# A chunked recurrent mixer regrouped on one Trainium2 core: one chunk and both head parities per group, level products on 64x64 quarters

## The chip, the cores and the metric

The kernel runs on one core of one Trainium2 chip. The metric is the device time of one execution in microseconds (us). Three executions of the kernel before took 1795.15, 1797.66 and 1800.07 us; the median is 1797.66.

## The reference

Four mixing layers of width 2048 run over 256 positions, all in float32. The first layer is the one that the change touches. It projects the input (`hn @ w_in`), computes a sparse attention for 8 heads on one part of the columns, and on another part a recurrence over time for 16 heads of width 64 with a state of 64 by 64 per head:

```python
def step(state, inp):
    r_t, w_t, k_t, v_t, a_t, b_t = inp
    sa = jnp.einsum('bhij,bhj->bhi', state, a_t)
    state = (state * w_t[:, :, None, :] + sa[..., None] * b_t[:, :, None, :]
             + v_t[..., None] * k_t[:, :, None, :])
    return state, jnp.einsum('bhij,bhj->bhi', state, r_t)
...
mix = jnp.concatenate([o_a * jax.nn.silu(z_a), o_b * jax.nn.silu(z_b)], axis=-1)
y = mix @ w_out[l]
```

The later layers (a differential attention and a gated linear attention, with their projections) are the same in both kernels.

## The kernel before

Six weight products (an input and an output projection for three layers) make up most of the work. `Gemm` cuts each into chunks of 256 columns and each chunk into four pieces of 512 KB. SyncE loads a piece, ScalarE rounds it (`hi`, L208), VectorE makes the remainder (`lo`, L213), and TensorE runs three matmuls for each *slot*: one 128-row slice of the contraction and one 128-wide tile of the output (L241 to L243, or L250 to L252). A piece of 256 columns has 8 slots. The input projection of the first layer has 992 slots.

Everything else is cut into *stages* that are woven into these slots. Each engine runs a generator that yields at each stage (`pe_stages`, `act_stages`, `dve_stages`), and a table `at` that `stage_slots` fills (L753) gives the slot before which stage n is issued, the same for all three engines. So a table of slots, and no scheduler, sets the order on every engine's queue; semaphores do the rest. Stages whose slot number lies past the last slot are issued after the projection, one after the other (`drained`). The sparse attention has its own table, `nsa_slots` (L351), which starts from the end of the recurrent stages (`at[-5]`): its first stage lies 16 slots behind it, and its last 229 slots behind it. In the kernel before the recurrent stages end at slot 834, so the attention's table runs from 850 to 1063; 17 of its stages lie past slot 992.

The recurrent mixer works in chunks of 128 positions (two chunks, `ch` 0 and 1) and on 8 heads at a time (`hh` 0 and 1). Four tiles `u` of 128 channels hold two heads each: the head of parity 0 on partitions 0 to 63, that of parity 1 on 64 to 127. For each `hh` there is a preparation (16 stages), then two groups of 36 stages, then 4 closing stages. A group takes one parity and *both* chunks; its stages alternate between chunk 0 and chunk 1, and lie 3 slots apart. In a group, for each of the 4 heads of that parity:

- `products` (L1003) makes five 128x128 matrices from 64-row operands: two whose masked parts NL and MU, MT start an inversion, and AK, RB, RK.
- The inversion of a 128x128 triangular matrix goes in `LV` = 6 levels. Each level doubles the size of the diagonal blocks that are inverted (b = 2, 4, ... 64) by two products. The first is NL times the odd block columns of MU (L1042), masked into QQ by VectorE (L1357). The second is MT, the transpose of MU, times QQ (L1052), which VectorE adds to MU (L1367). From level 1 on, TensorE also transposes MU (L1035) and ScalarE copies the result into MT (L1205). At levels 0 to 4 all products use the whole array: weights of 128x128, and 128 (levels 0 and 1) or 64 moving columns. Level 5 joins the two 64x64 halves and uses one 64x64 part (L1030, L1039, L1052).
- The output stages: AK times the values (L1064), MU times that (L1070), the state after chunk 0 (L1078, L1079, L1373 on VectorE), and the result (L1082, L1086, L1088). Chunk 1 also multiplies with the state (L1061, L1082).

Each float32 matmul of these is two instructions in the profile (a weight load and a matmul twice), called *runs* below. The stages that belong together are a *half-stage* of one chunk each:

```python
for lv in range(LV):
    for c in range(2):
        pe.wait_ge(dv_[c], d0[c] + 8 + 2 * lv)
        ...
        yield
    for c in range(2):
        pe.wait_ge(dv_[c], d0[c] + 9 + 2 * lv)
        ...
        yield
```

After the last group, `k.half_done` reaches 2 and SyncE may load the attention's weights and bias tables over the mixer's room. The gate values of the attention half (`za`) go through Silu on ScalarE before its heads start (L569 to L578); those of the recurrent half (`z2`, L1130) follow their projection chunks, and GpSimd multiplies them in (L1480). The block of the first layer ends with a barrier of all engines; then the next layer starts with a rounding of its operand (L1565, L1569) and its first pieces.

## Time and profile before

| what | value |
|---|---|
| median of 3 executions | 1797.66 us |
| the profiled execution: span from first to last instruction | 1793.7 us |
| TensorE busy (matmul) | 1719.0 us, 96% |
| VectorE / ScalarE busy | 1002.4 / 788.1 us |
| mean granted clock of TensorE | 0.981 |
| matmul instructions | 13621 |

The profiled execution's own time is given by its span alone; the median of the executions is 3.96 us longer than that span. The page gives busy time by engine, the granted TensorE clock in slices, DMA queues, the chain that ended last, and the costliest groups of instructions. Since matmuls are pipelined, one that is listed with 1.05 us can be followed by the next after 0.81 us; what a piece of work costs TensorE is read from start to start in the timeline.

### The profile page before, as it was taken

What the parts mean: (1) busy time and instruction counts of PE and PEld (TensorE: products, weight loads), DVE (VectorE), ACT (ScalarE), POOL (GpSimd) and SP (SyncE); (2) the same over time, 40 slices, a digit from 0 to 9 for tenths busy, and PEclk for the clock granted to TensorE, in tenths of its full rate; (3) what the DMA queues carried; (4) which work ended last, traced back from release to release, by engine and by line L of the source; (5) the groups of instructions that cost most, each with busy time, mean ns of one, the idle gap of its engine ahead of it and who ended that gap; (6) DMA issues with size and microseconds to landing.
All of it is one profiled execution on the core that took longest, in us unless ns stands there. A gap on an engine that the chain in (4) does not pass through costs nothing. (4 is left out here: it accounts for less than half of the span.)

```text
span 1793.7 us, 31345 instructions
## 1 busy us (share of the span) xinstructions
PE 1719.0 (96%) x13621; PEld 1639.8 (91%) x13621; DVE 1002.4 (56%) x1273; ACT 788.1 (44%) x1123; POOL 97.4 (5%) x88
## 2 busy tenths in 40 slices
PE   8999999899999898979999999999899999999899
PEld 7989998799998798978999989999898999999899
DVE  5665443664545265466454468887545854455443
ACT  6542223522222355444343348876436434444432
POOL 2210000300000000031000000000011000000000
PEclk9999999899999999989999999999999999999999
DMA  9643232433234915536666534444554655556363
GB/s 283 188 127 94 72 95 60 126 98 92 74 95 120 201 48 172 176 105 174 182 178 168 155 118 139 144 142 153 160 165 135 186 163 146 154 161 181 129 202 104
DMA packets 253584, 254.00 MB, mean 142 GB/s; under 512 B 9153, under 2 KB 249826, under 8 KB 253064
## 3 DMA queue, kind: packets, MB, share of 16 engines
q1 hardware_dynamic: 252792, 251.80, 47.9%
q8 instruction: 107, 1.75, 0.4%
q0 software_dynamic: 656, 0.21, 0.1%
q14 instruction: 29, 0.24, 0.0%
HBM read 249.29 MB, written 2.69 MB: 140 GB/s over the span
## 5 line engine op out<-in xcount | busy, mean ns | idle before, releaser
L213 DVE TENSOR_TENSOR w_lo<-w_raw,w_hi 128x1024 fp32r<-128x1024 f32 (+1 forms) x452 | 550.2, 1220 | 534.1 <-ACT w_hi L208 533.5
L241 PE MATMUL ps<-xt,w_hi 128*128 128x256 f32 x2736 | 805.8, 295 | 24.4 <-DVE w_lo L213 20.5
L242 PE MATMUL ps<-xt,w_hi 128*128 128x256 f32 x2736 | 779.7, 285 | 0.0
L243 PE MATMUL ps<-xt,w_lo 128*128 128x256 f32 x2736 | 779.2, 285 | 0.0
L208 ACT ACTIVATE w_hi<-w_raw 128x1024 fp32r<-128x1024 f32 (+1 forms) x452 | 470.2, 1045 | 667.1 <-PE ps L243 514.9
L241 PEld LDWEIGHTS ps<-xt,w_hi 128*128 128x128 f32 x2736 | 530.0, 194 | 49.5 <-issue 34.8
L242 PEld LDWEIGHTS ps<-xt,w_hi 128*128 128x128 f32 x2736 | 530.6, 194 | 1.2 <-issue 0.7
L243 PEld LDWEIGHTS ps<-xt,w_lo 128*128 128x128 f32 x2736 | 529.9, 194 | 0.0
L250 PE MATMUL ps<-w_hi,xt 128*128 128x256 f32 x832 | 244.0, 293 | 0.0
L251 PE MATMUL ps<-w_lo,xt 128*128 128x256 f32 x832 | 236.8, 285 | 0.0
L252 PE MATMUL ps<-w_hi,xt 128*128 128x256 f32 x832 | 236.6, 284 | 0.0
L250 PEld LDWEIGHTS ps<-w_hi,xt 128*128 128x128 f32 x832 | 161.2, 194 | 8.9 <-issue 7.8
L251 PEld LDWEIGHTS ps<-w_lo,xt 128*128 128x128 f32 x832 | 161.3, 194 | 0.5 <-issue 0.2
L252 PEld LDWEIGHTS ps<-w_hi,xt 128*128 128x128 f32 x832 | 160.9, 193 | 0.0
L319 DVE TENSOR_TENSOR proj<-ps,rs_bc 128x512 f32<-128x512 f32 (+1 forms) x71 | 48.0, 676 | 54.0 <-PE ps L243 53.8
L1052 PE MATMUL ps<-arena 128*128 128x64 f32 (+2 forms) x384 | 46.4, 263 | 0.0
L1052 PEld LDWEIGHTS ps<-arena 128*128 128x128 f32 (+1 forms) x384 | 43.6, 182 | 1.1
L1357 DVE TENSOR_TENSOR arena<-ps,con 128x256 f32<-128x256 f32 (+1 forms) x40 | 21.2, 530 | 38.6 <-PE ps L1042 38.4
L1205 ACT ACTIVATE arena<-ps 128x512 f32<-128x512 f32 x32 | 19.0, 595 | 53.5 <-PE ps L1035 53.3
L1765 ACT ACTIVATE df_sc<-df_sc,df_st 128x128 f32<-128x128 f32 x64 | 28.4, 445 | 7.7 <-DVE df_st L1841 7.6
L1866 DVE RECIPROCAL t_sq<-t_sq 128x256 f32<-128x256 f32 x16 | 27.9, 1746 | 1.0 <-ACT t_sq L1779 1.0
L1472 POOL COPY arena<-con 8x512 f32<-8x512 f32 x2 | 1.3, 667 | 389.7 <-PE ps L1097 389.7
(395 smaller groups left out, 1531.4 us busy)
## 6 DMA issues: line engine op xcount, KB each, us to landing
w_raw<-in_a_w_in SPq DMA_DIRECT2D x128, 512.0 KB, 3.7
w_raw<-in_w_in SPq DMA_DIRECT2D x120, 512.0 KB, 3.6
w_raw<-in_b_w_in SPq DMA_DIRECT2D x96, 512.0 KB, 3.7
w_raw<-in_w_out SPq DMA_DIRECT2D x32, 512.0 KB, 4.2
w_raw<-in_a_w_out SPq DMA_DIRECT2D x32, 512.0 KB, 4.5
w_raw<-in_b_w_out SPq DMA_DIRECT2D x32, 512.0 KB, 3.5
arena<-in_x SPq DMA_DIRECT2D x4, 512.0 KB, 7.1
w_raw<-in_w_in SPq DMA_DIRECT2D x8, 256.0 KB, 3.8
```

Source lines behind the costliest of these rows:

```text
L208: k.nc.scalar.activation(k.wh[:, p % RING, :, 0:w], k.raw[:, p % RAW, :, 0:w], ACT.Copy).then_inc(k.hi_made, 1)
L213: k.nc.vector.tensor_tensor(k.wl[:, p % RING, :, 0:w], k.raw[:, p % RAW, :, 0:w], k.wh[:, p % RING, :, 0:w].bitcast(F32), ALU.subtract).th ...
L241: pe.matmul(os, h[:, cs], xt[:, kt, 0:S], start=st and ct == 0, stop=False, skip_group_check=True)
L242: pe.matmul(os, h[:, cs], xt[:, kt, S:2 * S], start=False, stop=False, skip_group_check=True)
L243: last = pe.matmul(os, l[:, cs], xt[:, kt, 0:S], start=False, stop=sp, skip_group_check=True)
L250: pe.matmul(os, xh, h[:, 0:w], start=st and tt == 0, stop=False, skip_group_check=True)
L251: pe.matmul(os, xh, l[:, 0:w], start=False, stop=False, skip_group_check=True)
L252: last = pe.matmul(os, xl, h[:, 0:w], start=False, stop=sp, skip_group_check=True)
L319: k.nc.vector.tensor_tensor(spec["dst"], g.bank(c)[:, 0:nt * S].rearrange("p (j t) -> p j t", j=nt), view(k.rsb[:, 0:1], [[0, nt], [1, S]] ...
L1052: m = pe.matmul(share(bank(c, 0), u, lv)[half, :], unit(buf[c][MT], u)[half, half], share(buf[c][QQ], u, lv)[half, :], start=True, stop=True)
L1765: nc.scalar.activation(sc[:, i % 2, t, rows[tt]], sc[:, i % 2, t, rows[tt]], ACT.Exp, bias=st[:, i % 2, 0, t, tt:tt + 1], accum_out=st[:, ...
L1866: nc.vector.reciprocal(rh, rh).then_inc(l4, 1)
```

## The change

- **Groups.** A group now takes one chunk and both parities: chunk 0 first, then chunk 1. It has 18 stages instead of 36, and each stage does for parity 0 and 1 what two stages did for chunk 0 and 1. The gaps between stages come from `GROUP_GAPS` (3, 2, 3, 9, then fourteen of 5): 87 slots for a group instead of 108. The recurrent stages end at slot 750 instead of 834, and the attention's table runs from 766 to 979.
- **Products.** The products from 64-row operands take parity 0 and 1 in turn, into two PSUM banks. RK, AK and RB are made in two further banks (4 and 5) by `side_products`: RK before the levels, AK behind the second half of level 1, RB behind the second half of level 3.
- **Levels 0 to 4** work on the two diagonal 64x64 quarters `q` of each matrix: two matmuls with 64 rows and 64 weight columns instead of one with 128 and 128. The quarter q = 0 uses rows 0 to 63 and writes partitions 0 to 63, q = 1 uses and writes 64 to 127, in the same PSUM bank. The moving columns are 64 at levels 0 and 1 and 32 at levels 2 to 4. On VectorE the masked copy into QQ covers 256 or 128 columns, and the addition into MU becomes two operations of 64 partitions for each parity.
- **Level 5 and the output stages** keep their products; matmuls of the two parities that write 64 partitions each now alternate.
- **The gates** `za` of the attention go through Silu later: the first four heads' before the first head, the other four within the stages of head 2.
- The constants array loses 575 columns, most of them masks (`K_END`).

```diff
-LV, ODD = 6, 2
 R_LORA, R_RVK, R_ZB = 0, 1, 28
-N_PE = tuple(5 + 3 * LV - 1 + 4 - c for c in range(2))
-N_DVE = tuple(8 + 2 * LV + 1 - c for c in range(2))
+LV = 6
+G_PE = tuple(2 + 3 * LV - 1 + 4 - ch for ch in range(2))
+G_DVE = tuple(5 + 3 * LV - 1 + 1 - ch for ch in range(2))
 N_ACT = LV - 1 + 3
+GROUP_GAPS = (3, 2, 3, 9) + (5,) * (2 * LV - 1) + (5, 5, 5)
...
-        for _ in range(2 * (12 + 4 * LV)):
-            now += 3
+        for gap in GROUP_GAPS + GROUP_GAPS:
+            now += gap
...
+        def gated(f):
+            za = k.proj[:, T_ZA + 4 * f:T_ZA + 4 * f + 4, :]
+            act.wait_ge(k.evac_d, self.za_done[f])
+            nc.scalar.activation(za, za, ACT.Silu).then_inc(self.zs, 1)
...
+            def products(banks, lhs, rhs, done):
                 for u in range(4):
-                    m = pe.matmul(bank(c, y)[:, u * P:(u + 1) * P], lhs[ps_, u, cs], rhs[ps_, u, cs],
-                                  start=True, stop=True)
-                m.then_inc(mm_[c], 1)
-
-            for c in range(2):
-                if par == 0:
-                    pe.wait_ge(ev, 6 * hh + 6)
-                if n:
-                    pe.wait_ge(dv_[c], d0[c])
-                    pe.wait_ge(ac_[c], a0)
-                products(c, 0, at_(hh), bt(hh))
-                products(c, 1, bt(hh), at_(hh))
-                yield
-            for c in range(2):
-                pe.wait_ge(dv_[c], d0[c] + 3)
-                products(c, 0, pk, at_(hh))
-                products(c, 1, bt(hh), pr)
-                yield
-            for c in range(2):
-                pe.wait_ge(dv_[c], d0[c] + 6)
-                products(c, 0, pk, pr)
-                yield
+                    for par in range(2):
+                        ps_ = rows_of(par)
+                        m = pe.matmul(banks(par)[:, u * P:(u + 1) * P], lhs[ps_, u, cs], rhs[ps_, u, cs],
+                                      start=True, stop=True)
+                        if u == 3:
+                            m.then_inc(done[par], 1)
+
+            def side_products(i, lhs, rhs):
+                for par in range(2):
+                    if 3 * n + i:
+                        pe.wait_ge(sd_[par], 3 * n + i)
+                products(side_bank, lhs, rhs, sp_)
...
+            products(lambda par: bank(par, 0), at_(hh), bt(hh), mm_)
+            yield
+            products(lambda par: bank(par, 1), bt(hh), at_(hh), mm_)
+            yield
+            side_products(0, pk, pr)
+            yield
...
-                            m = pe.matmul(share(bank(c, 0), u, lv), unit(buf[c][NL], u),
-                                          columns_of(buf[c][MU], u, lv), start=True, stop=True)
-                    m.then_inc(mm_[c], 1)
-                    yield
...
+                        w = LQ_W[lv]
+                        for q in range(2):
+                            m = pe.matmul(bank(par, 0)[rows_of(q), u * w:(u + 1) * w], diagonal(b[NL], u, q),
+                                          odd_columns(unit(b[MU], u), q, lv, P, 1), start=True, stop=True)
+                    m.then_inc(mm_[par], 1)
+                yield
...
-                        m = pe.matmul(share(bank(c, 0), u, lv)[half, :], unit(buf[c][MT], u)[half, half],
-                                      share(buf[c][QQ], u, lv)[half, :], start=True, stop=True)
...
+                        w = LQ_W[lv]
+                        for q in range(2):
+                            m = pe.matmul(bank(par, 0)[rows_of(q), u * w:(u + 1) * w], diagonal(b[MT], u, q),
+                                          b[QQ][rows_of(q), u * w:(u + 1) * w], start=True, stop=True)
+                    m.then_inc(mm_[par], 1)
+                if lv == 1:
+                    side_products(1, pk, at_(hh))
+                elif lv == 3:
+                    side_products(2, bt(hh), pr)
...
-                        nc.vector.tensor_tensor(all_columns(b[MU], lv), all_columns(b[MU], lv),
-                                                packed(bank(c, 0), lv), ALU.add).then_inc(dv_[c], 1)
...
+                    for q in range(2):
+                        to = odd_columns(b[MU], q, lv, P, 4)
+                        nc.vector.tensor_tensor(to, packed(bank(par, 0), q, lv), to, ALU.add).then_inc(dv_[par], 1)
+                if lv == 1:
+                    side(1, AK, up)
+                elif lv == 3:
+                    side(2, RB, upi)
```

Three places show how the instructions move. The first is TensorE at level 2 of the first group (con: the identity, for transposes; proj and arena: NL and MU, MT, QQ of the two matrices of a stage; ps: PSUM; the semaphores dv0 and dv1 come from VectorE, ac0 and ac1 from ScalarE). Before, with nine projection matmuls at each "...":

```order
L1035 MATMUL ps<-con,proj 128x128 [waits rwc_dv0]
L1035 MATMUL ps<-con,proj 128x128 x3
L1042 MATMUL ps<-proj 128x64 x4
...
L1035 MATMUL ps<-con,arena 128x128 [waits rwc_dv1]
L1035 MATMUL ps<-con,arena 128x128 x3
L1042 MATMUL ps<-arena 128x64 x4
...
L1052 MATMUL ps<-arena 128x64 [waits rwc_ac0,rwc_dv0]
L1052 MATMUL ps<-arena 128x64 x3
...
L1052 MATMUL ps<-arena 128x64 [waits rwc_ac1,rwc_dv1]
L1052 MATMUL ps<-arena 128x64 x3
```

Now, with fifteen at the "...":

```order
L1063 MATMUL ps<-con,proj 128x128 [waits rwc_dv0]
L1063 MATMUL ps<-con,proj 128x128 x3
L1063 MATMUL ps<-con,arena 128x128 [waits rwc_dv1]
L1063 MATMUL ps<-con,arena 128x128 x3
L1074 MATMUL ps<-proj 64x32 x8
L1074 MATMUL ps<-arena 64x32 x8
...
L1090 MATMUL ps<-arena 64x32 [waits rwc_ac0,rwc_dv0]
L1090 MATMUL ps<-arena 64x32 x7
L1090 MATMUL ps<-arena 64x32 [waits rwc_ac1,rwc_dv1]
L1090 MATMUL ps<-arena 64x32 x7
```

Four half-stages of one chunk became two of both parities, and each product with 128x128 weights became two with 64x64 weights. The second place is VectorE at the same level (w_lo is the remainder of a weight piece). Before:

```order
L1357 TENSOR_TENSOR arena<-ps,con 128x256 [waits rwc_mm0]
L1357 TENSOR_TENSOR arena<-ps,con 128x256 [waits rwc_mm1]
L1367 TENSOR_TENSOR proj<-proj,ps 128x32x8 [waits rwc_dv0,rwc_mm0]
L213 TENSOR_TENSOR w_lo<-w_raw,w_hi 128x1024 [waits hi_made]
L1367 TENSOR_TENSOR arena<-arena,ps 128x32x8 [waits rwc_dv1,rwc_mm1]
```

Now:

```order
L1415 TENSOR_TENSOR arena<-ps,con 128x128 [waits rwc_mm0]
L1415 TENSOR_TENSOR arena<-ps,con 128x128 [waits rwc_mm1]
L1429 TENSOR_TENSOR proj<-ps,proj 64x4x4x8 [waits rwc_mm0]
L1429 TENSOR_TENSOR proj<-ps,proj 64x4x4x8
L1429 TENSOR_TENSOR arena<-ps,arena 64x4x4x8 [waits rwc_mm1]
L1429 TENSOR_TENSOR arena<-ps,arena 64x4x4x8
```

The masked copy is half as wide, and each addition is two operations on 64 partitions. The third place is TensorE at the end of the first layer (L459: transposes of the attention's weights of one head; L469, L473, L474: its values product; the row before the branch ends the block). Before, the first row being the last matmul of the input projection:

```order
L243 MATMUL ps<-xt,w_lo 128x256
L449 MATMUL ps<-proj 128x128 [waits nsa_pre]
...
L469 MATMUL ps<-arena 128x256 [waits nsc_te]
...
L459 MATMUL ps<-con,arena 128x128 [waits nsa_pte,nsa_nrm]
L459 MATMUL ps<-con,arena 128x128 x5
L469 MATMUL ps<-arena 128x256 [waits nsa_mxd,nsc_te]
L473 MATMUL ps<-arena,proj 128x256 [waits nsa_pte]
L474 MATMUL ps<-arena,proj 128x128
L473 MATMUL ps<-arena,proj 128x256
L474 MATMUL ps<-arena,proj 128x128
L1403 UNCONDITIONAL_BRANCH
```

Now:

```order
L476 MATMUL ps<-arena,proj 128x256 [waits nsa_pte]
L477 MATMUL ps<-arena,proj 128x128
L476 MATMUL ps<-arena,proj 128x256
L477 MATMUL ps<-arena,proj 128x128
L244 MATMUL ps<-xt,w_hi 128x256
...
L246 MATMUL ps<-xt,w_lo 128x256
L1468 UNCONDITIONAL_BRANCH
```

The last head's products, which ended the block, are issued 36 projection matmuls before its end.

## Rows read from the trace of the kernel before

**Rows 1.** Page: span, and section 1, busy time and share of each engine

```profile
span 1793.7 us, 31345 instructions
...
PE 1719.0 (96%) x13621; PEld 1639.8 (91%) x13621; DVE 1002.4 (56%) x1273; ACT 788.1 (44%) x1123; POOL 97.4 (5%) x88
```

**Rows 2.** Busy us of PE, PEld, DVE, ACT, POOL, PEclk, DMA, GB/s: first group

```profile
128.86:214.93 86.07, 86.07 (x734) 82.58 (x733) 41.37 (x59) 22.61 (x30) 0.00 (x0) 1.00 0.31 88
```

**Rows 3.** Timeline of PE, steady input projection: start, duration, line, shapes, count

```profile
1061.40 0.28 PE L252 MATMUL ps<-w_hi,xt 128*128 128x256 f32 x1
1061.52 0.28 PE L250 MATMUL ps<-w_hi,xt 128*128 128x256 f32 x1
```

**Rows 4.** Timeline of PE, first group

```profile
128.86 2.05 PE L1003 MATMUL ps<-proj 64*128 64x128 f32 x16
...
132.11 2.05 PE L1003 MATMUL ps<-proj 64*128 64x128 f32 x16
...
152.37 1.06 PE L1052 MATMUL ps<-arena 128*128 128x128 f32 x8
...
154.33 0.60 PE L1035 MATMUL ps<-con,proj 128*128 128x128 f32 x4
...
156.74 0.60 PE L1035 MATMUL ps<-con,arena 128*128 128x128 f32 x4
...
191.61 0.41 PE L1030 MATMUL ps<-con,arena 64*64 64x64 f32 x4
...
193.82 0.68 PE L1052 MATMUL ps<-arena 64*64 64x64 f32 x8
...
195.69 0.67 PE L1052 MATMUL ps<-arena 64*64 64x64 f32 x8
...
201.50 0.33 PE L1078 MATMUL ps<-proj 128*64 128x64 f32 x2
...
201.78 0.28 PE L1078 MATMUL ps<-proj 128*64 128x64 f32 x2
...
202.37 0.28 PE L1079 MATMUL ps<-proj 128*64 128x64 f32 x2
...
205.59 1.10 PE L1061 MATMUL ps<-rw_state,proj 64*128 64x64 f32 x8
...
208.70 1.00 PE L1070 MATMUL ps<-proj,arena 128*128 128x64 f32 x8
```

**Rows 5.** Timeline of PE: whole-array products, and two 64-row halves into two banks

```profile
651.73 0.60 PE L450 MATMUL ps<-proj 128*128 128x256 f32 x2
...
652.16 0.39 PE L449 MATMUL ps<-proj 128*128 128x128 f32 x2
...
1061.97 0.50 PE L1701 MATMUL ps<-proj 64*128 64x128 f32 x4
...
1062.19 0.31 PEld L1702 LDWEIGHTS ps<-proj 64*128 64x128 f32 x4
...
1062.84 0.38 PE L250 MATMUL ps<-w_hi,xt 128*128 128x256 f32 x1
```

**Rows 6.** Timeline of PE: two 64-column halves in one bank

```profile
1484.46 1.51 PE L2168 MATMUL ps<-gl_qd,proj 128*64 128x256 f32 x16
...
1485.90 0.39 PE L250 MATMUL ps<-w_hi,xt 128*128 128x256 f32 x1
```

**Rows 7.** Groups of DVE by form, third group: count, busy us, mean ns, idle before

```profile
L213 DVE TENSOR_TENSOR w_lo<-w_raw,w_hi 128x1024 fp32r<-128x1024 f32 x13 | 15.9, 1223 | 14.8 <-ACT w_hi L208 14.8
...
L319 DVE TENSOR_TENSOR proj<-ps,rs_bc 128x512 f32<-128x512 f32 x3 | 2.1, 688 | 6.9 <-PE ps L243 6.9
...
L1373 DVE TENSOR_TENSOR rw_state<-ps,rw_fac 64x256 f32<-64x256 f32 x1 | 0.4, 417 | 1.6 <-PE ps L1079 1.6
```

**Rows 8.** Timeline: end of the first layer on POOL, ACT and PE

```profile
663.24 1.27 POOL L1480 TENSOR_TENSOR proj<-proj 128x512 f32<-128x512 f32 x1 [16.25 <-ACT proj L1130]
...
662.53 0.63 ACT L1130 ACTIVATE proj<-proj 128x512 f32<-128x512 f32 x1
...
689.87 0.55 PE L241 MATMUL ps<-xt,w_hi 128*128 128x256 f32 x1 [4.70 <-DVE w_lo L213]
```

More of the change, by code:

```diff
@@ L936, in pe_stages @@
                 yield from pe_prepare(pe, hh)
[L937 to L938 removed]
+                for ch in range(2):
+                    yield from pe_group(pe, 2 * hh + ch)
                 yield from pe_finish(pe, hh)
@@ L1037, in pe_group @@
+                for par in range(2):
+                    b = buf[par]
                     for u in range(4):
                         if lv == LV - 1:
[L1039 to L1043 removed]
@@ L1062, in pe_group @@
+                yield
+            for par in range(2):
+                pe.wait_ge(dv_[par], d0 + dv_at(LV) - 1)
+                pe.wait_ge(sd_[par], 3 * n + 2)
+            for u in range(4 * ch):
+                for par in range(2):
+                    ps_ = rows_of(par)
+                    pe.matmul(bank(par, 0)[:, u * 64:(u + 1) * 64], at_(hh)[ps_, u, cs], state[ps_, u, :],
                               start=(u == 0), stop=False, skip_group_check=True)
+            for par in range(2):
@@ L1090, in pe_group @@
-                m.then_inc(mm_[c], 1)
-                yield
+                    m = pe.matmul(bank(par, 0)[:, u * 64:(u + 1) * 64], unit(buf[par][AK], u), tok(aa, ch, u, par),
+                                  start=(ch == 0 and u == 0), stop=True, skip_group_check=True)
+                m.then_inc(mm_[par], 1)
+            yield
+            for par in range(2):
+                pe.wait_ge(ac_[par], a0 + LV)
+                for u in range(4):
+                    m = pe.matmul(bank(par, 1)[:, u * 64:(u + 1) * 64], unit(buf[par][MU], u),
+                                  xu(par)[:, u * 64:(u + 1) * 64], start=True, stop=True)
+                m.then_inc(mm_[par], 1)
```

363 lines of the change are left out of this document (191 added, 172 removed).

## The prediction

> **What bounds the kernel now.** I read the page's busy times first, then the windows of one group of the mixer, then the timeline of TensorE. On the page TensorE is busy for 1719.0 of 1793.7 us, 96% [rows 1]. In the first group it is busy for all of its 86.07 us at a granted clock of 1.00 (the 2.4 GHz level), while VectorE works 41.37 us, 48%, and ScalarE 22.61 us [rows 2]. So in the groups the time is TensorE's own work, and I can count instructions. A projection matmul starts 0.12 us after the one before it [rows 3]; a slot of three is 0.36 us. The 36 stages of a group lie 3 slots apart, 38.9 us of projection. The other 86.1 - 38.9 = **47.2 us** are the mixer's, and there are four groups. The projection's 992 slots stay, so what the mixer saves, the layer saves.
>
> The price of one half-stage is the distance from one stage to the next less nine projection matmuls (1.08 us) [rows 4]:
> - 16 runs of 64-row products: 132.11 - 128.86 = 3.25, so 2.17 us.
> - 8 runs with 128x128 weights: 154.33 - 152.37 = 1.96, so 0.88.
> - transposes and first product: 156.74 - 154.33 = 2.41, so 1.33. Apart they would cost about 0.45 + 0.88.
> - level 5: 2.21 (191.61 to 193.82), so 1.13 with the transposes, and 1.87 (193.82 to 195.69), so 0.79 without.
> - output: 4.09 (201.50 to 205.59), so 3.01, and 3.11 (205.59 to 208.70), so 2.03.
>
> Within such a stage, ten runs with 64 weight columns and 64 moving columns take from 201.78 to 202.37, 0.059 each [rows 4]; a run with 128x128 weights takes 0.11. About 0.3 us of each stage is thus no run at all but the change between projection and mixer.
>
> **The change, part by part.** Its main question is whether two runs on different quarters of the array go side by side. Whole-array runs of 256 columns take 0.215 us each (two from 651.73 to 652.16), half that for 128 columns. Two 64-row halves into two banks do overlap: four 128-column runs have gone when the fifth's weights load, 1062.19 - 1061.97 = 0.22 us instead of 0.43, and with four more of 256 columns the stage takes 0.87 us instead of 1.30 [rows 5]. Weight loads overlap there too. Two 64-column halves in one bank overlap as well: 16 runs with 2560 columns in all take 1.44 us instead of 2.15 [rows 6]. No row has two row halves in *one* bank, which is what the quarters of levels 0 to 4 do. I price a pair of quarters at one run of 0.058 us, since they differ in rows as in rows 5 and in columns as in rows 6; the bound below is a gain of nothing more, the bound above is two runs, 0.116.
>
> The Trainium skill (TensorEngine Tiling (Array Packing), Restrictions and Gotchas, Gotcha 1) says that different row tiles can't access the same PSUM bank simultaneously. By that rule the pairs at levels 0 to 4 would go one after the other, and the sum would be rival A's. Rows 5 agree with the part of it that two banks work; no row here shows one bank with two row tiles.
>
> Per group, both parities together:
> - Products: 3 stages of 16 runs in pairs over two banks. 2.17 - 8 x 0.115 = 1.25, taken as 1.3 each: 3.9 us. Two more hang on levels 1 and 3 without a change of kind of their own: 2 x 1.15 = 2.3. Before: 10 half-stage products.
> - Level 0: two stages of 16 pairs. The row for 8 runs is 0.79; 8 more of 0.058 make 1.26. Two: 2.5.
> - Levels 1 to 4: the first stage adds 8 transposes (0.89) to 1.26. When two kinds share a stage some 0.15 is saved: 1.3 + 0.89 against the 2.03 of the output row. So 2.0, and 1.26 for the second: 3.26 x 4 = 13.0.
> - Level 5: 1.13 + 12 x 0.058 = 1.83, then 1.26: 3.1.
> - Output: AK 1.7, MU 1.7 (16 whole-array runs each), and the last 3.0, where column halves of the parities go side by side: 6.4. Chunk 1 has one product more with the state (+1.15) and 3.1: 7.7 in all.
>
> That is 31.2 us for a group of chunk 0 and 32.5 for chunk 1, 31.85 on average against 47.2: 15.35 less, times four = **-61.4 us**.
>
> What it costs:
> - *Start of a group.* VectorE masks and copies the products for both parities in the first stages: ten operations of 128x512 at 0.69 us and one or two remainders of weights at 1.22 [rows 7], together 8.1 to 9.3 us. TensorE has meanwhile 3 + 2 + 3 + 9 slots (6.1 us) and about 4 us of stages, less where the first operation can start, 8.9 us in all. I take 1 us a group, **+4**; the bounds are 0 and 3 us a group. Projection chunks are evacuated by operations of 0.69 us as well [rows 7], and where one falls in, it is the upper bound.
> - *Levels.* Between two stages of a group lie 5 slots, 1.8 us. VectorE has then two masked copies (256 or 128 columns, at most 0.42 each by the row of 256 columns) or four half additions (at most 4 x 0.42 = 1.7), and one remainder in some of them. Before, two stages of 3 slots each gave 2.16 us and another stage between. I take 0; the chance of more is rival C. VectorE's work in a group stays near 39 us by these durations, of 63: 62%.
> - *Attention stages.* Seventeen were issued after the last slot and now lie within the projection. TensorE was busy in nearly all of them, so they are moved, not saved; each costs a return to the projection of about 0.1 us: **+1.4**.
> - *End of the layer.* The attention's last products hid the last projection chunk: its evacuation (0.69), Silu (0.63) and GpSimd's multiplication of 1.27 us [rows 7, 8]. Now they follow the last matmul in the open, and what follows them is the 4.70 us that TensorE already waits before its first matmul of the output projection [rows 8]. Of these 2.6 us, 0.4 us stood in the open before: **+2.2**, bounds 0 and 4.
> - *Silu among the heads* on ScalarE: two more of 0.63 us and their changes of function; the heads' stages now have projection slots behind them. **+1**, bounds 0 and 3.
> - SyncE's later loads (`half_done`, then the attention's weights and bias) keep their distance in slots to the attention's table, which moves up by 84 slots with them; the projection's pieces come at the pace of its slots, and DMA engines were 31% busy in a group [rows 2]. A projection slot comes 10% sooner in a group at most. Zero; if that cover went, a late piece would show as a wait on `w_raw`. The fewer constants are loaded ahead and worth zero, bound -1.
>
> Sum: -61.4 + 4 + 1.4 + 2.2 + 1 = -52.8. Against the profiled execution's 1793.7 us of span that is 1740.9; the median is 3.96 us above that span, so **1745 us**. The group becomes 87 x 0.36 + 31.85 = 63.2 us long.
>
> **Rivals.**
> - *A. Quarters don't go side by side* (they share a bank, or no run starts sooner than 0.058 us after another; the change then doesn't do what it says). Levels 0 to 4 have 10 stages of 16 pairs, 160 a group: 160 x 0.058 x 4 = +37.1 us, 1782. For it: no row has it; the fastest sequence shown is 0.059 a run. Against it: the start of four runs within 0.22 us with weights of 128 columns [rows 5], and rows 6 for one bank. Chance 0.17.
> - *B. A part of it*: pairs at 0.09 us, as the 1.44 us of rows 6 are more than half of 2.15. 160 x 0.032 x 4 = +20, 1765. Chance 0.08.
> - *C. VectorE becomes the chain* (slower than before). In each level TensorE waits for additions or copies behind a remainder of 1.22 us: four of 0.42 and 1.22 are 2.9 us against 1.8 of slots. A group has 12 such hand-overs, 48 in all; at 52.8 / 48 = 1.1 us each the gain is gone. At 2 us each it is 1745 + 96 = 1841. Against it: a remainder comes once in 8 slots, so not in each stage; VectorE was 48% busy, and additions that are half or a quarter as wide are cheaper than the 0.42 taken. Chance 0.05 for slower, 0.04 for a stop near zero.
>
> **How the numbers follow.** The forecast has 0.66, with a range of its own of 1738 to 1756 (the bounds of the costs at the ends). The whole range has to take in A, so it runs from 1735 to 1785, and leaves out C and a little below. 0.3% of 1797.66 is 5.4 us, about what a measurement of this kernel can tell from no change. Faster: forecast, A and B, 0.91; same 0.04; slower 0.05.
>
> **What would show it.** Right: stages of quarters about 1.3 us longer than the fifteen projection matmuls (1.8 us) before the next; a group 63 us long with TensorE busy in nearly all of it; the first matmul of the output projection some 7 us behind the last of the input projection, with no attention stage between. Wrong: stages of quarters 2.2 us beyond their slots (A); idle time of TensorE in the groups released by VectorE (C), above all behind the first three stages; attention stages that wait for ScalarE; a group of over 70 us. If the groups are short and the time is not, the loss lies at the layer's end.

## The result and the profile after

Four executions of the changed kernel took 1741.67 to 1748.74 us, median **1747.41 us**; before it was 1797.2 us in the same comparison. The ratio is **0.9712**, 95% interval 0.9692 to 0.9731: faster by 2.9%, some 50 us. The forecast was 1745 us, in a range of 1735 to 1785.

The page of the changed kernel, against [rows 1]: the span and the line of busy times and shares.

```profile
span 1746.6 us, 32649 instructions
...
PE 1663.0 (95%) x14261; PEld 1582.2 (91%) x14261; DVE 996.7 (57%) x1313; ACT 793.7 (45%) x1128; POOL 96.8 (6%) x88
```

The span is 47.1 us shorter than before. TensorE is busy 56 us less though it has 640 matmul instructions more, and its share fell from 96 to 95%: part of what it saved came back as waiting.

Busy us of PE, PEld, DVE, ACT and POOL (with counts), PE's granted clock, DMA share and GB/s, in the first two groups of the mixer and in two stretches of the attention, as in [rows 2]:

```profile
128.70:191.89 63.19, 63.08 (x830) 59.25 (x830) 37.40 (x66) 19.13 (x27) 0.00 (x0) 1.00 0.32 100
...
191.89:257.35 65.46, 65.46 (x838) 61.26 (x839) 36.14 (x64) 19.44 (x28) 0.00 (x0) 1.00 0.30 90
...
520.00:540.00 20.00, 12.15 (x85) 10.84 (x84) 4.11 (x9) 4.31 (x9) 0.00 (x0) 0.82 0.91 161
...
540.00:560.00 20.00, 17.71 (x101) 16.88 (x100) 8.66 (x17) 5.26 (x13) 0.00 (x0) 0.67 0.28 86
```

The first group (chunk 0) takes 63.19 us and the second (chunk 1) 65.46, where a group took 86.07 [rows 2]. TensorE is busy in all but 0.11 us of them, at clock 1.00. VectorE's share rose from 48% to 59 and 55%. The last two rows are told of below.

The timeline of TensorE in the first group (start, duration, line, shapes, count), the rows that answer to [rows 4]:

```profile
128.70 1.16 PE L1029 MATMUL ps<-proj 64*128 64x128 f32 x16
...
130.70 1.16 PE L1029 MATMUL ps<-proj 64*128 64x128 f32 x16
...
137.58 0.68 PE L1074 MATMUL ps<-proj 64*64 64x64 f32 x16
...
140.65 1.15 PE L1090 MATMUL ps<-arena 64*64 64x64 f32 x32
...
143.63 0.60 PE L1063 MATMUL ps<-con,proj 128*128 128x128 f32 x4
...
147.66 1.15 PE L1090 MATMUL ps<-arena 64*64 64x64 f32 x32
...
151.72 0.60 PE L1063 MATMUL ps<-con,proj 128*128 128x128 f32 x4
...
155.73 1.12 PE L1090 MATMUL ps<-arena 64*64 64x32 f32 x32
...
158.68 0.60 PE L1063 MATMUL ps<-con,proj 128*128 128x128 f32 x4
...
180.36 1.90 PE L1108 MATMUL ps<-proj,arena 128*128 128x64 f32 x16
...
183.94 1.00 PE L1115 MATMUL ps<-proj 128*128 128x64 f32 x8
...
187.61 0.34 PE L1125 MATMUL ps<-proj 128*64 128x64 f32 x4
```

Between two of these stages stand 15 projection matmuls (1.8 us), after the first product six (0.72), between the last two rows 15 again. 128.70 to 130.70 gives 1.28 us for a product of both parities. A stage of quarters is 155.73 to 158.68, less 1.8: **1.15 us for 32 runs**, with 32 moving columns; with 64 it is 1.18 (140.65 to 143.63). The two quarters of a matrix thus run side by side, although they write one PSUM bank. The trace's single starts say it directly: from 155.81 to 156.63 the two runs of each pair start 0.007 us apart, and the next pair 0.058 us behind.

To see where the 47.1 us come from, I divide the first layer at the same stages in both timelines and set aside the slots, at 0.357 us each:

| stretch | before, us | after, us | slots before / after | difference beyond slots |
|---|---|---|---|---|
| groups 1 and 2 | 173.12 | 128.65 | 219 / 177 | -29.5 |
| closing stages and next preparation | 71.58 | 72.73 | 115 / 115 | +1.2 |
| groups 3 and 4 | 173.12 | 128.75 | 219 / 177 | -29.4 |
| from there to the output projection | 143.19 | 182.33 | 175 / 259 | +9.2 |

That is -58.9 us in the groups and +10.4 outside them; with 0.2 us before the first group the output projection starts 48.7 us earlier (641.16 against 689.87, [rows 8]). The later layers took 1.6 us longer in this execution, which is within what executions differ by.

The 10.4 us outside are mostly waits of TensorE. In the changed kernel (the bracket is idle time and its releaser):

```profile
303.58 1.88 PE L100 MATMUL ps<-proj,con 128*8 128x256 f32 x4 [6.76 <-ACT proj L1229]
...
538.50 0.80 PE L452 MATMUL ps<-proj 128*128 128x128 f32 x2 [7.85 <-DVE arena L629]
...
641.16 0.55 PE L244 MATMUL ps<-xt,w_hi 128*128 128x256 f32 x1 [6.90 <-DVE w_lo L216]
```

In the kernel before, the ones that answer to the first and second of these; the last has its row in [rows 8] (4.70):

```profile
347.14 2.10 PE L98 MATMUL ps<-proj,con 128*8 128x256 f32 x6 [2.63 <-ACT proj L1174]
...
622.46 0.80 PE L449 MATMUL ps<-proj 128*128 128x128 f32 x2 [5.19 <-DVE arena L623]
```

From the first group's start to the output projection all such waits add up to 31.5 us after and 22.7 before, the ones not shown among them (the largest, for a remainder ahead of the first, 3.77 us before and 2.53 after).

### The profile page after: what moved, and what is told of

Its sections match the earlier page's. It is cut to its first block and busy times, and to the rows that moved or that the text cites. A ratio compares the mean times of both kernels' runs of the same rounds, so it can differ in the third digit from the quotient of the medians.

```text
span 1746.6 us, 32649 instructions
## 1 busy us (share of the span) xinstructions
PE 1663.0 (95%) x14261; PEld 1582.2 (91%) x14261; DVE 996.7 (57%) x1313; ACT 793.7 (45%) x1128; POOL 96.8 (6%) x88
## 5 line engine op out<-in xcount | busy, mean ns | idle before, releaser
L244 PE MATMUL ps<-xt,w_hi 128*128 128x256 f32 x2736 | 803.4, 294 | 27.0 <-DVE w_lo L216 22.7
L1256 ACT ACTIVATE arena<-ps 128x512 f32<-128x512 f32 (+1 forms) x40 | 20.0, 549 | 36.6 <-PE ps L1063 29.2
L1429 DVE TENSOR_TENSOR proj<-ps,proj 64x128 f32<-64x128 f32 (+1 forms) x40 | 13.6, 340 | 16.6 <-PE ps L1090 16.0
L1090 PEld LDWEIGHTS ps<-arena 64*64 64x64 f32 x640 | 20.2, 134 | 2.8 <-DVE arena L1415 0.2
L333 ACT ACTIVATE proj<-ps,rs_tok 128x256 f32<-128x256 f32 x18 | 8.5, 470 | 31.3 <-PE ps L255 31.3
L1090 PE MATMUL ps<-arena 64*64 64x32 f32 (+1 forms) x640 | 22.6, 221 | 0.0
```

The source lines that it names most:

```text
L244: pe.matmul(os, h[:, cs], xt[:, kt, 0:S], start=st and ct == 0, stop=False, skip_group_check=True)
L1090: m = pe.matmul(bank(par, 0)[rows_of(q), u * w:(u + 1) * w], diagonal(b[MT], u, q), b[QQ][rows_of(q), u * w:(u + 1) * w], start=True, stop ...
```

## Experiments

Twelve variants of the changed kernel ran, in three sets; each set had runs of the kernel before on the same chip, so that their ratios stand beside the 0.9712 of the change. Stage times come from one profiled execution each, and carry most of the argument; medians of two variants that differ by under 5 us are not told apart by them.

### Do the quarters overlap, and does the bank matter?

**Quarters in rows.** Neighbours in the queue share a quarter:

```diff
-                    for u in range(4):
+                    for q, u in [(q, u) for q in range(2) for u in range(4)]:
...
-                        for q in range(2):
-                            m = pe.matmul(bank(par, 0)[rows_of(q), u * w:(u + 1) * w], diagonal(b[NL], u, q),
+                        m = pe.matmul(bank(par, 0)[rows_of(q), u * w:(u + 1) * w], diagonal(b[NL], u, q),
```

> At levels 0 to 4 the four products on quarter 0 are issued first, then the four on quarter 1, so neighbours share a quarter. Theory (neighbouring runs on different quarters overlap, a run alone costs 0.058 us): a stage of 32 runs goes from about 1.18 us beyond its slots to about 2.1 us, 10 stages in each of 4 groups, +37 us: about 1784 us. Rival (32 moving columns are short enough that the order doesn't matter at levels 2 to 4, only at levels 0 and 1): 4 of the 10 stages, +15 us: about 1762. Second rival (the queue of TensorE looks ahead, so order doesn't matter): no change, 1747.

Measured: 1760.17 us, ratio 0.9801 (0.9787 to 0.9816). The timeline of TensorE at level 0 (the view breaks a group of runs where another one's interleave with it):

```profile
137.83 0.27 PE L1074 MATMUL ps<-arena 64*64 64x64 f32 x1
...
137.89 0.22 PE L1074 MATMUL ps<-proj 64*64 64x64 f32 x1
...
140.71 1.54 PE L1090 MATMUL ps<-arena 64*64 64x64 f32 x32
...
144.06 0.60 PE L1063 MATMUL ps<-con,proj 128*128 128x128 f32 x4
```

No expectation held. The median agrees with the first rival's 1762, but not for its reason: the stage grows at 64 columns from 1.18 to 1.55 us (140.71 to 144.06) and at 32 columns nearly as much, from 1.15 to 1.46. All 40 stages grow, by 13.3 us in all (135.26 and 135.44 us for two groups, against 257.40 for the four). Why they don't double is in the rows: the line 137.83 (matrix of parity 1, quarter 0) starts before the line 137.89 (parity 0, quarter 1), which stands ahead of it in the queue. Runs on a free quarter start ahead of waiting ones, so even groups of four matmuls overlap at their borders. In the trace's single starts each eight runs begin when five of the eight before them have started, so three runs ahead. This edit didn't measure a run without overlap, which called for the next one.

**One quarter.** Both products of a pair use quarter 0; quarter 1 of the level products is left out.

```diff
-                            m = pe.matmul(bank(par, 0)[rows_of(q), u * w:(u + 1) * w], diagonal(b[NL], u, q),
+                            m = pe.matmul(bank(par, 0)[rows_of(0), u * w:(u + 1) * w], diagonal(b[NL], u, 0),
...
```

> At levels 0 to 4 both products of a pair use quarter 0 (the same number of runs, shapes and bytes); quarter 1 of the level products is left out and the output of the recurrent half differs. With the quarters issued in rows of four the stage grew only from 1.18 to 1.55 us beyond its slots, which I read as runs on another quarter starting ahead of waiting ones. Theory (without another quarter to go to, 32 runs cost 0.058 us each whatever the moving columns, 64 or 32): 1.86 + 0.1 us in place of 1.18, +0.78 x 40 stages = +31 us: about 1778 us, and whole_array (16 runs at 0.10) comes out below it. Rival (the 32-column runs of levels 2 to 4 are cheaper alone, 0.03 us): only the 16 stages of levels 0 and 1 grow, +13 us: 1760.

Measured: 1783.88 us, ratio 0.9920 (0.9904 to 0.9937), 36 us above the change. Two stages, with 64 and 32 moving columns:

```profile
141.20 2.08 PE L1090 MATMUL ps<-arena 64*64 64x64 f32 x32
...
145.11 0.60 PE L1063 MATMUL ps<-con,proj 128*128 128x128 f32 x4
...
159.99 2.05 PE L1090 MATMUL ps<-arena 64*64 64x32 f32 x32
...
163.87 0.38 PE L1063 MATMUL ps<-con,proj 128*128 128x128 f32 x2
```

141.20 to 145.11 is 2.11 us beyond the slots, 159.99 to 163.87 is 2.08: 32 runs at 0.06 us and the return, whatever the columns. So a run on 64x64 weights costs 0.06 us alone, and the pair costs the same: side by side the two quarters are worth 0.93 us x 40 stages = **37 us**. The groups grew by 18.4 us a pair of groups (147.02 against 128.65), 36.8 in all. That is the price of rival A in the prediction, now measured.

**Banks alternate.** The two parities take turns, so that a neighbour on the other quarter writes another bank:

```diff
-                for par in range(2):
-                    b = buf[par]
-                    for u in range(4):
+                for u in range(4):
+                    for q, par in ((0, 0), (1, 1), (0, 1), (1, 0)):
...
```

> Same runs as the changed kernel, but at each level stage the two parities alternate, so that a neighbour on the other quarter writes another PSUM bank. Theory (a shared bank costs nothing): the stages keep 1.15 to 1.18 us, the time stays at 1747 within 3 us; a stage that now waits for both parities before it starts may add up to 0.1 us where VectorE is close behind. Rival (the shared bank costs a part of the overlap): the stages fall below 1.1 us, by up to 0.1 us x 40 = 4 us in all.

Measured: 1746.32 us, ratio 0.9729 (0.9712 to 0.9746). The second stage of level 2, and the stage after it:

```profile
155.35 1.12 PE L1090 MATMUL ps<-arena 64*64 64x32 f32 x32
...
158.31 0.60 PE L1063 MATMUL ps<-con,proj 128*128 128x128 f32 x4
```

155.35 to 158.31 is 2.96 us against 2.95 in the change. One shared bank costs nothing here: the two runs of a pair start 0.007 us apart in both traces, here into two banks, in the change into one.

The Trainium skill (TensorEngine Tiling (Array Packing), Restrictions and Gotchas, Gotcha 1) says that different row tiles can't access the same PSUM bank simultaneously. Had the pairs gone one after the other by that rule, as the prediction read it, the changed kernel would have taken the time of the one-quarter run. The measurement decides otherwise for quarters that differ in rows and in columns, and so write other partitions: 1.15 us for 32 runs into one bank, and 1.16 with two. Two row tiles that write the same partitions of one bank weren't tried.

**Whole array.** One product with 128x128 weights in place of two on quarters; the other quarter's rows and columns are multiplied in as well:

```diff
-                        for q in range(2):
-                            m = pe.matmul(bank(par, 0)[rows_of(q), u * w:(u + 1) * w], diagonal(b[NL], u, q),
-                                          odd_columns(unit(b[MU], u), q, lv, P, 1), start=True, stop=True)
+                        m = pe.matmul(bank(par, 0)[:, u * w:(u + 1) * w], unit(b[NL], u),
+                                      whole_columns(unit(b[MU], u), lv), start=True, stop=True)
...
```

> Levels 0 to 4 use one product with 128x128 weights in place of two on quarters; everything else as in the changed kernel. The rows and columns of the other quarter are multiplied in as well, so the output of the recurrent half differs; the work on the other engines is the same. Theory: 16 runs at 0.11 us are 1.76 us, and with 0.1 for the return 1.85 beyond the slots in place of 1.18, +0.67 x 40 stages = +27 us: about 1774 us. Then of the 59 us that the four groups saved some 27 are the quarters' and some 32 the regrouping's. Rival (regrouping is worth little by itself): 1790 or more.

Measured: 1765.87 us, ratio 0.9837 (0.9817 to 0.9857), 18 us above the change; in the profile the groups take 21.8 us more (139.55 + 139.68 against 257.40).

```profile
142.41 1.90 PE L1094 MATMUL ps<-arena 128*128 128x64 f32 x16
...
145.99 0.60 PE L1069 MATMUL ps<-con,proj 128*128 128x128 f32 x4
...
150.44 1.90 PE L1094 MATMUL ps<-arena 128*128 128x64 f32 x16
```

142.41 to 145.99 is 1.78 us beyond the slots in place of 1.18. So of the 58.9 us some **22 are the quarters'** and **37 the regrouping's**: fewer returns to the projection, and pairs in the other products (at least 10.8, by the next run). I had expected 27 and 32. The runs do start 0.11 us apart, as I had it, but the stage takes 1.78 us and not 1.85, and a stage that begins with transposes grows least: 2.65 us (145.99 to 150.44) against 2.21 with quarters. The same eight transposes thus add 0.87 us ahead of whole-array products and 1.06 ahead of quarters. Serial quarters (one quarter, +37) are worse than whole products (+22): without overlap this split would have been a loss against whole products in the same groups.

**Parities apart.** In the products from 64-row operands all of parity 0 stand before parity 1:

```diff
-                for u in range(4):
-                    for par in range(2):
+                for par in range(2):
+                    for u in range(4):
```

> In the products from 64-row operands all four of parity 0 come before all four of parity 1. Theory (the pair is worth 8 x 0.115 us): each of the 5 stages of a group goes from 1.09 to 2.0 us, +0.9 x 5 x 4 = +18 us: about 1765 us. Rival (the gain of these stages came from fewer returns to the projection): no change, 1747.

Measured: 1757.19 us, ratio 0.9782 (0.9765 to 0.9798).

```profile
128.19 1.71 PE L1029 MATMUL ps<-proj 64*128 64x128 f32 x16
...
130.73 1.71 PE L1029 MATMUL ps<-proj 64*128 64x128 f32 x16
```

128.19 to 130.73 less 0.72 is 1.82 us in place of 1.28: +0.54, not +0.9, and 20 stages make 10.8 us; the groups grew by 10.8 (134.11 twice, against 128.65 and 128.75). Issued one after the other, the halves of four matmuls overlap at their border as the quarters in rows did, again by three runs. The pairing is worth something, as the theory had it; its size with the order undone was over-estimated by the same mechanism.

### How near is VectorE to its limit?

**Gaps of 4 and of 3.** Stages of the levels 4 or 3 slots apart; the attention's table is fixed at its slots of the changed kernel (766 and 810):

```diff
-GROUP_GAPS = (3, 2, 3, 9) + (5,) * (2 * LV - 1) + (5, 5, 5)
+GROUP_GAPS = (3, 2, 3, 9) + (4,) * (2 * LV - 1) + (5, 5, 5)
...
-    now = at[-5] + NSA_WAIT
-    out = [at[-5] + 16]
+    now = 810
+    out = [766]
```

> Stages of the levels lie 4 slots apart instead of 5; the attention's table stays where it was. Theory (in the groups TensorE is never kept waiting by VectorE, and its work is the same): no idle time in a group, the time stays at 1747 within 4 us. Rival (the level chain is at its limit with 5 slots): a wait behind each of some 20 stages, 0.3 us or more each, +6 us or more.

Measured: 1739.72 us, ratio 0.9692 (0.9677 to 0.9706), so about 8 us better than the change, and outside of what either theory gave.

```profile
334.81 1.15 PE L1090 MATMUL ps<-arena 64*64 64x64 f32 x32 [1.43 <-DVE arena L1415]
...
489.64 0.58 PE L244 MATMUL ps<-xt,w_hi 128*128 128x256 f32 x1 [3.72 <-DVE w_lo L216]
```

Two groups take 121.16 us. They have 22 slots fewer, 7.85 us; the rest is 0.36 us more than before. The third and fourth group take 122.41 us, 1.5 us more than the slots explain, with the wait of 1.43 us in the third. So the theory about the groups holds but for that one wait. The gain is elsewhere, and I had changed two things: with the heads at a fixed slot, the recurrent half ends 44 slots earlier and the bias tables' transfers start earlier. The 7.85 us at slot 853 are gone; 3.72 us at a remainder are new.

> Stages of the levels lie 3 slots apart (1.07 us). Between two stages VectorE needs 2 x 0.3 to 0.4 us and the hand-over both ways, and 1.22 us more where a remainder falls in. Theory (the slack of 5 slots is about 1 us a hand-over): waits of up to 1.2 us behind a remainder, about one in three stages, +5 to +15 us: about 1757. Rival (large slack): no change, 1747.

Measured: 1753.83 us, ratio 0.9762 (0.9745 to 0.9778).

```profile
140.59 1.15 PE L1090 MATMUL ps<-arena 64*64 64x64 f32 x32 [0.50 <-DVE arena L1415]
```

The groups now show waits on VectorE of 0.2 to 0.5 us at levels 0, 1 and 5, and take 3.1 us more than their slots explain, so 6 us for all four. That was the expected mechanism at the low end of its price; between 5 slots and the limit lies about one slot. Behind the groups four waits for a remainder (3.58, 0.90, 0.63 and 2.24 us) took the place of the 7.85 us before the first head. The time fell in the range that I gave, and the groups account for it.

### The waits outside the groups

**Heads 20 slots later.**

```diff
-NSA_A, NSA_WAIT = 5, 60
+NSA_A, NSA_WAIT = 5, 80
```

> The attention's stages from the third on come 20 slots later, so the last three lie past the projection's end. Theory (TensorE waits 7.85 us for the bias tables because the head stages come by slot and the tables by time, and 6.90 us at the layer's end because nothing covers the last gates): the first wait goes, the second falls to about 4.7 us, both together -7.85 - 2.2 and +1 for stages in the tail: about 1738 us. Rival (the same transfers hold up the weight pieces behind them, so the wait comes back at the next remainder): 1745 to 1747.

Measured: 1739.05 us, ratio 0.9688 (0.9671 to 0.9705). The wait before the output projection:

```profile
631.93 0.36 PE L244 MATMUL ps<-xt,w_hi 128*128 128x256 f32 x1 [4.55 <-DVE w_lo L216]
```

The output projection starts at 631.93 instead of 641.16, 9.2 us earlier. All waits together fell by 9.4 us (31.5 to 22.2): the 7.85 and 2.35 that the theory names are gone, and on balance 0.8 came back at others: a remainder waits 3.52 us at 506.04 in place of 1.73 at 493.34, and a later head's stage 2.12 us at 571.48. The wait for the tables was a stage that came too early by its slot.

**Last head 24 slots later.**

```diff
-    for _ in range(NSA_H):
+    for n in range(NSA_H):
+        now += 24 * (n == NSA_H - 1)
```

> Only the last head's three stages come 24 slots later, past the last slot. Theory (of the 6.90 us before the output projection's first matmul some 2.2 are the last projection chunk's evacuation, Silu and multiplication, which these stages cover): the wait falls to 4.5 to 5 us, -2 us: about 1745 us. Rival (the wait is the load and rounding of the output projection's first piece and of its operand, in any case): 6.9 us stay behind the last stage, +2.5 us for stages that lose their cover: about 1750.

Measured: 1742.34 us, ratio 0.9703 (0.9689 to 0.9718).

```profile
636.81 0.42 PE L244 MATMUL ps<-xt,w_hi 128*128 128x256 f32 x1 [4.54 <-DVE w_lo L216]
```

The wait at the layer's end falls from 6.90 to 4.54 us, within what was expected; the wait for the tables is still there (7.14). The median fell by 5 us rather than 2; the difference lies within the spread of executions.

**Preparation 20 slots later.**

```diff
-                           (end(c + 4), 4), (end(c + 5), 4), (0, 4), (0, 8), (0, 10), (0, 3), (0, 8), (0, 10), (0, 5)):
+                           (end(c + 4), 4), (end(c + 5), 4), (0, 4), (0, 8 + 20 * hh), (0, 10), (0, 3), (0, 8), (0, 10), (0, 5)):
```

> The stage of the second half's preparation before which TensorE waits 6.76 us for ScalarE comes 20 slots later, and all stages behind it, the attention's too, which so ends at slot 999. Theory (each of these waits is a stage that its slot brings too early, and every slot ahead of it is paid for anyway): that wait goes; at the end of the layer 6.90 falls to about 4.6; the 7.85 us before the first head stays, since its distance to the last recurrent stage does: 1747 - 6.8 - 2.3 + 1 = about 1739 us. Rival (ScalarE is busy with rounding for those slots, so the wait moves with the stage or comes back at a remainder): 1745 to 1747.

Measured: 1737.57 us, ratio 0.9659 (0.9638 to 0.9679).

```profile
312.36 1.77 PE L995 MATMUL ps<-arena 8*128 8x256 f32 x7 [1.29 <-DVE arena L1346]
```

The 6.76 us are gone, but 0.28, 1.61, 0.55 and 1.29 us stand in their place (three remainders and a VectorE result): from the end of the second group to the start of the third it is 75.85 us, 3.1 more for 20 slots more, which are 7.1; the gain there is 4.0 us, between theory and rival. The end of the layer gave its 2.4 us again (4.54), and the attention's other waits are some 2 us shorter (31.5 to 22.7 in all). So the time came out as expected by another split; the profiled execution was the fastest of the four (1731.8 us), so its stages can be a little shorter than in the median.

**Gaps of 4, heads from slot 830**, both edits from above (766 and 830).

> Gaps of 4 slots in the levels and the attention's heads from slot 830 (before: 810), so that three stages lie past the last slot. gaps_4 alone gave 1739.7 us with the wait of 7.85 us gone, because its recurrent half ended 44 slots before the heads' fixed place. Theory: the 6.87 us at the end falls to about 4.6 and nothing else changes: about 1738 us. Rival (gaps_4 is faster for a cause within the groups): no more than that either, but then the stages of the groups are shorter in gaps_4 than in the changed kernel.

Measured: 1735.81 us, ratio 0.9657 (0.9641 to 0.9674), the lowest median, 3.4% under the kernel before and beneath the change by more than both intervals.

```profile
631.53 0.55 PE L244 MATMUL ps<-xt,w_hi 128*128 128x256 f32 x1 [4.54 <-DVE w_lo L216]
```

The end fell to 4.54 us as expected. Before slot 800 a remainder still costs 2.36 and 2.24 us.

**Combined**: gaps of 4, the preparation's stage 20 slots later, heads from 830.

> Gaps of 4 slots, the preparation's stage 20 slots later and the heads from slot 830: all three waits (6.76 us in the preparation, 7.85 us before the first head, 2.3 of the 6.90 at the end) are given cover. Theory: 1747.4 - 6.8 - 7.9 - 2.3 + 1 for stages in the tail + 1 to 3 for waits in the groups at 4 slots = 1733 us. Rival (weight pieces and remainders follow in the same time and the waits come back there, as 3.72 us at slot 784 in gaps_4): 1737 to 1740.

Measured: 1739.75 us, ratio 0.9675 (0.9653 to 0.9697), no better than its parts.

```profile
307.79 2.07 PE L995 MATMUL ps<-arena 8*128 8x256 f32 x4 [3.97 <-DVE arena L1346]
```

The rival was right. The wait in the preparation moved one stage on (3.97 us, on VectorE), and from group 2's end to group 3's start it takes 78.34 us with 20 slots more than the change: only 1.5 us are gained there. VectorE came to L1346 behind two long remainders (the second pair of rows is GpSimd at the same time):

```profile
299.19 3.79 DVE L216 TENSOR_TENSOR w_lo<-w_raw,w_hi 128x512 fp32r<-128x512 f32 x1
...
302.91 2.85 DVE L216 TENSOR_TENSOR w_lo<-w_raw,w_hi 128x512 fp32r<-128x512 f32 x1
```

```profile
300.04 2.39 POOL L1532 TENSOR_TENSOR arena<-arena,proj 128x1024 f32<-128x1024 f32 x1
302.51 2.70 POOL L1535 TENSOR_TENSOR arena<-arena 128x1024 f32<-128x1024 f32 x1
```

The same operation takes 0.62 us with GpSimd idle (at 307.66), so these two cost VectorE 5.4 us more; in the run with the preparation alone they took 2.27 and 3.44 us (304.71 and 306.89). In all fourteen traces each remainder of over 1.4 us has a GpSimd operation beside it. That the two engines hinder each other is read from this; no run moved GpSimd's work away. Remainders at slots 776, 800, 832 and 840 wait 4.1 us together, and there the weights' transfers are late too: ScalarE waits 10.16 us for a piece before 482.51. Once the early stages have cover, it is the weights that come late, by their transfers and by VectorE.

## Why the prediction was right, step by step

**The groups.** The sum gave -61.4 us of TensorE work and +4 for the start of a group, so -57.4; measured were -58.9. The two came close because two errors cancelled: the work fell by 58.9 and not 61.4, and the start of a group cost nothing. Single terms, of the first group:

| stage | predicted, us | measured, us |
|---|---|---|
| product of both parities | 1.3 | 1.28 |
| the same inside a level | 1.15 | 1.08 (147.66 to 151.72, less 2.98) |
| level 0, second product | 1.26 | 1.18 |
| levels 1 to 4, first stage | 2.0 | 2.21 |
| levels 1 to 4, second | 1.26 | 1.15 to 1.24 |
| level 5 | 1.83 + 1.26 | 1.82 + 1.17 |
| AK, MU, result | 1.7, 1.7, 3.0 | 1.78, 1.87, 3.20 |

The pair of quarters at one run's price was the step on which most hung. It held, and its alternative was priced rightly: rival A's +37.1 us, by the one-quarter run 36.8. Rival B's part-overlap is excluded by the same rows. The saving of 0.15 us where transposes and products share a stage didn't show: 2.21 is 1.15 + 1.06. The price of 0.89 for the transposes holds ahead of whole-array products (0.87 in the whole-array run), and ahead of quarters they cost 0.19 more. One reading of rows 5 was loose: 0.22 us is when the fifth weight load starts, which runs ahead of the matmuls. From the first of the four matmuls to the fifth it is 0.33 us by the single starts (1061.97 to 1062.30), the first 0.21 of them up to the second pair; that halves overlap stands.

**Start of a group: +4 predicted, 0 measured.** The ten operations of 128x512 came as counted. In the fourth group:

```profile
394.39 1.23 DVE L216 TENSOR_TENSOR w_lo<-w_raw,w_hi 128x1024 fp32r<-128x1024 f32 x1 [2.47 <-ACT w_hi L211]
...
395.53 0.68 DVE L1389 TENSOR_TENSOR proj<-ps,con 128x512 f32<-128x512 f32 x1
...
396.13 0.68 DVE L1390 TENSOR_TENSOR arena<-ps,con 128x512 f32<-128x512 f32 x1
```

They start 0.60 us apart though each is listed with 0.68, so VectorE needs 6.0 us where I had 6.9, and with the remainder ahead of them (1.14 to the next start) is done at 401.6; the next stage of TensorE that needs its results starts 8.9 us behind the group's start (137.58 against 128.70 in the first group), here at 402.3. The step read durations where it should have read distances from start to start, which I had done for TensorE alone.

**Levels on VectorE: 0 predicted.** Right, with a narrow margin. The busy time of the first group is 37.4 us; I had 39.

```profile
L1429 DVE TENSOR_TENSOR proj<-ps,proj 64x128 f32<-64x128 f32 x6 | 1.7, 286 | 2.2 <-PE ps L1090 2.1
```

A half addition at 32 columns per matrix is 0.29 us, not 0.42. Gaps of 4 slots cost 0.4 us in the first pair of groups and 1.5 in the second, gaps of 3 cost 3.1 in each. Rival C was far in price (it wanted 1.1 us at each of 48 hand-overs), but a change of two slots in the table would have begun it.

**End of the layer: +2.2 predicted, +2.2 measured** (6.90 against 4.70). Its chain in the changed kernel, on VectorE, ScalarE, GpSimd and ScalarE again:

```profile
634.29 0.69 DVE L322 TENSOR_TENSOR proj<-ps,rs_bc 128x512 f32<-128x512 f32 x1 [3.88 <-PE ps L246]
...
635.02 0.63 ACT L1185 ACTIVATE proj<-proj 128x512 f32<-128x512 f32 x1 [7.77 <-DVE proj L322]
...
635.73 1.26 POOL L1545 TENSOR_TENSOR proj<-proj 128x512 f32<-128x512 f32 x1 [15.67 <-ACT proj L1185]
...
637.42 1.06 ACT L1630 ACTIVATE xt<-proj 128x1024 fp32r<-128x1024 f32 x1 [1.77 <-PEq L1468]
```

Evacuation, Silu and multiplication end at 636.99; only then does the barrier let the rounding for the output projection (L1630) begin. With three stages of a head in the tail the wait is 4.54, so this chain is shown to be the 2.3 us.

**Attention and transfers: 1.4 + 1 + 0 predicted, 7.0 measured** (9.2 less the 2.2 at the end), and 1.2 more between the groups, where I had none. This is the term that was mis-sized. I wrote of SyncE's later loads that they "keep their distance in slots" and gave them zero. The first head's stage waits for the last bias tables, before and after:

```profile
619.21 0.19 DVE L667 COPY cbias<-arena 128x35 f32<-128x35 f32 x1 [8.52 <-DMA proj<-bias_rows_dram]
```

```profile
535.85 0.19 DVE L673 COPY cbias<-arena 128x35 f32<-128x35 f32 x1 [17.69 <-DMA proj<-bias_rows_dram]
```

After, VectorE is idle for 17.69 us until this copy, and TensorE, whose stage came by its slot, has waited 7.85 us by 538.50 (5.19 before, by 622.46). The distance did keep, in slots and nearly in time: from SyncE's first load of the attention's weights to TensorE's arrival at the stage it is 51.95 us before (565.32 to 617.27) and 51.30 after (479.35 to 530.65). It was too short in both, and the transfers took longer: from that load to the copy 53.89 us before and 56.50 after. So the shorter cover explains at most 0.65 us of the growth of 2.66; why the transfers took 2.6 us longer is not shown. In the seven variants that leave this distance alone the wait is 6.04 to 10.42 us, so one execution doesn't fix its size.

All waits in this stretch, the end aside, are 14.5 us after and 10.1 before, which is 4.4 of the 7.0. TensorE's clock is most of the rest. In the windows of 520 to 560 us it was granted 0.82 and then 0.67, a mix of its levels of 2.4 and 1.2 GHz, behind a stretch in which it was busy for 12.15 of 20 us (before, 0.74 in the window of 620 to 640). From the first head's stage to the output projection TensorE was busy at 1.2 GHz for 14.4 us after and 8.7 before. Projection matmuls start 0.21 us apart there (541.65, 541.87, 542.08) and 0.12 at 2.4 GHz, so 5.7 us more at the lower level cost some 2.5 us, by estimate. That leaves nearly nothing for the returns to the projection and the Silu, which I had put at 1.4 and 1. In the 1.2 us between the groups the waits grew by 2.2 us (7.9 to 10.1), and less time at 1.2 GHz gave a part back.

**The total.** -52.8 was predicted for the span, -47.1 measured: -1.5 by the groups, +4.6 in the attention, +1.2 in the preparation, +1.6 in the later layers. The median came nearer (1747.4 to 1745) because the span lay 0.8 us under the median of the runs and not the 4 us that I had carried over. That part is luck: for the span, which the sum was about, the miss is 5.7 us, and for the median only 2.4.

## What to carry to other kernels

Small products that use a half or a quarter of TensorE should be issued so that neighbours in the queue use different rows of it, and for parts on the diagonal one PSUM bank will do; without a partner, a split into quarters is slower than the whole array. A table of slots gives each stage a distance in matmuls, whatever the stage waits for: look for the stages whose releaser is a DMA or another engine's fixed work, and move those. Here this took away the waits of 7.85 and 6.76 us, though part of them came back elsewhere. Read the price of every engine's work from start to start, and don't change a gap and what is anchored to it in one experiment.

## What was not expected

- Runs of 64x64 weights cost 0.06 us each with 32 and with 64 moving columns (2.08 and 2.11 us for 32 of them with the return). Narrow levels are bound by the number of runs.
- TensorE starts runs on a free quarter ahead of others that stand before them in the queue. It does so by up to three runs. With eight runs of one quarter in a row the stage takes 1.55 us, between 1.18 (alternating) and 2.11 (no overlap).
- VectorE's operations of 128x512 follow each other every 0.60 us, listed with 0.68 each.
- The remainders of 128x512 that VectorE makes in 0.62 us alone took up to 3.79 us with a GpSimd operation beside them. In the combined schedule two of them cost VectorE 5.4 us just ahead of the stage that TensorE waits for.
- Transposes on the whole array cost 0.19 us more a stage when products on quarters follow them than when whole-array products do.
